# Forty instead of thirty-two tokens by gathered expert rows, with two VectorE dots in every body of the spread

## The reference

```python
q = (t @ w_pq).reshape(n_tok, 8, 2, 128)
sc = einsum('thcd,hckd->thck', q, sub_keys)            # 128 keys in each half
top_s, top_i = top_k(sc, 16)                            # then the 16 best of the 16 x 16 sums
expert_idx, gate = ...                                  # 8 heads x 16 picks of 16384 experts
a = gelu(einsum('thkd,td->thk', expert_u[expert_idx], t))
out = einsum('thk,thkd->td', gate * a, expert_v[expert_idx])
x = rms_norm(x + out)
```

## Time and profile before

| | |
|---|---|
| median of three runs | 2140.78 us |
| the profiled execution's own time | 2139.2 us |
| its span from first to last instruction | 2137.2 us |
| granted TensorE clock, mean | 0.997 |
| TensorE matmul busy | 2108.7 us (99%) |
| TensorE weight load busy | 1973.4 us (92%) |
| VectorE busy | 1584.1 us (74%) |
| ScalarE busy | 1118.9 us (52%) |
| GpSimd busy | 488.8 us (23%) |
| DMA, mean | 226 GB/s |

### The profile page before, as it was taken

The page is one execution under the profiler, slowest core; times in us unless marked ns, Lnnn a source line. Parts: engine busy times, 40 slices in busy tenths (PEclk is TensorE's granted clock), DMA queues, the critical chain, the costliest instruction groups (busy, mean ns, idle before and its releaser), DMA issues.

```text
span 2137.2 us, 40878 instructions
## 1 busy us (share of the span) xinstructions
PE 2108.7 (99%) x13494; PEld 1973.4 (92%) x13494; DVE 1584.1 (74%) x2622; ACT 1118.9 (52%) x1879; POOL 488.8 (23%) x379
## 2 busy tenths in 40 slices
PE   8999999999999999999999999999999999999997
PEld 6888888889989999999999999999999999999997
DVE  6555566667777986888778888888777776777775
ACT  5444455446455655556555555555555554555553
POOL 0000000000000000001999999332222220111110
PEclk9999999999999999999999999999999999999998
DMA  7655554445556556666767666888877776877773
GB/s 246 235 187 190 183 166 157 149 155 189 181 192 230 166 174 210 207 210 224 228 221 222 222 221 222 286 309 313 312 286 291 285 283 215 267 275 266 268 251 128
DMA packets 134750, 482.26 MB, mean 226 GB/s; under 512 B 15455, under 2 KB 18399, under 8 KB 134295
## 3 DMA queue, kind: packets, MB, share of 16 engines
q1 hardware_dynamic: 116072, 414.29, 57.6%
q0 software_dynamic: 18432, 67.12, 8.8%
q10 hardware_dynamic: 174, 0.05, 0.0%
HBM read 477.16 MB, written 4.24 MB: 225 GB/s over the span
## 4 chain that ended last, share of the span: by engine, by line
PE 95%; DVE 3%; issue 1%; DMA 1%; ACT 0%; DVEq 0%; SPq 0%; ACTq 0%
PE ps L1643 35%; PE ps L1912 19%; PE ps L1650 19%; PE ps L1916 11%; PE ps L1673 5%; PE ps L1896 2%; DVE lo L1014 1%; PE ps L1767 1%; PE ps L1749 1%; PE ps L1758 0%; DMA raw<-w_down 0%; DMA x_t<-x_t 0%; DVE score_b L1322 0%; DVE idx_now L1324 0%; DVE top_now L1328 0%
## 5 line engine op out<-in xcount | busy, mean ns | idle before, releaser
L1014 DVE TENSOR_TENSOR lo<-raw,hi 128x1024 fp32r<-128x1024 f32 x760 | 935.3, 1231 | 473.5 <-PE ps L1643 144.5
L622 ACT CAST hi<-raw 128x1024 fp32r<-128x1024 f32 x760 | 795.7, 1053 | 346.8 <-DMA raw<-w_down 137.6
L1643 PE MATMUL ps<-move_u,hi 128*128 128x448 f32 x2048 | 451.1, 368 | 0.0
L1912 PE MATMUL ps<-act_now,hi 128*128 128x448 f32 x2048 | 439.8, 365 | 0.4 <-ACT hi L622 0.4
L1912 PEld LDWEIGHTS ps<-act_now,hi 128*128 128x128 f32 x2048 | 375.0, 188 | 26.4 <-issue 0.7
L1643 PEld LDWEIGHTS ps<-move_u,hi 128*128 128x128 f32 x2048 | 371.0, 189 | 24.6
L1643 PE MATMUL ps<-move,hi 128*128 128x512 f32 x1536 | 379.3, 395 | 9.5 <-ACT hi L622 9.5
L1643 PEld LDWEIGHTS ps<-move,hi 128*128 128x128 f32 x1536 | 281.5, 189 | 62.9 <-issue 9.5
L630 ACT COPY upper<-ps 128x224 f32<-128x224 f32 (+1 forms) x224 | 80.3, 358 | 484.3 <-PE ps L1643 484.2
L602 POOL TENSOR_SCALAR one_j<-iota,j_t,gate_t 128x128 f32<-128x128 f32 x224 | 296.8, 1331 | 3.0 <-ACT j_t L880 1.8
L1916 PEld LDWEIGHTS ps<-act_now,lo 128*128 128x128 f32 x2048 | 250.6, 191 | 7.3 <-DVE lo L1014 2.0
(11 more groups left out here) (206 smaller groups left out, 1628.2 us busy)
## 6 DMA issues: line engine op xcount, KB each, us to landing
raw<-w_u SPq DMA_DIRECT2D x256, 512.0 KB
raw<-w_down SPq DMA_DIRECT2D x256, 512.0 KB
raw<-w_qk SPq DMA_DIRECT2D x68, 512.0 KB
raw<-w_gate SPq DMA_DIRECT2D x64, 512.0 KB
raw<-w_out SPq DMA_DIRECT2D x32, 512.0 KB
raw<-w_pq SPq DMA_DIRECT2D x32, 512.0 KB
raw<-w_v SPq DMA_DIRECT2D x28, 512.0 KB
raw<-w_o SPq DMA_DIRECT2D x24, 512.0 KB
```

Of the source, the lines that this page charges most:

```text
L622: nc.scalar.copy(hi[slot][:], raw[slot][:]).then_inc(hi_ready, 1)
L1014: nc.vector.tensor_tensor(lo[s % LOS][:], raw[s % RAW][:], hi[s % RAW][:].bitcast(F32), ALU.subtract).then_inc(lo_ready, 1)
L1643: ins = nc.tensor.matmul(ps[bank][:, 0:2 * w], hi[slot][:, col:col + P], m, start=begins, stop=ends)
L1912: return nc.tensor.matmul(ps[d][:, 0:2 * TD], hi[s % RAW][:, d * P:(d + 1) * P], act_now[s % ACTS][:], start=begins, stop=ends)
```

## The change

S becomes 40. That makes TD = 216, COPIES = 3 (three copies of 40 tokens, NP = 120 partitions), PICKS = 43 and STEPS = 86, PAIRS = 108 and UG = 51, so the spread has 27 bodies. A gather fetches 120 rows. Three `rows` buffers are used in turn instead of two. The dots stand in slot 3 of bodies 22 and 23, then in slots 1 and 3 of every body from 24 on, which is up to body 65, the second body of the down stage. GpSimd issues gather 2 before pair 0 and gather 3 before pair 1, and from then on gather g before pair 2g - 5, so two in every body of the spread. A gather of step g now waits for the dot of g - 3. The 43 adds of each half are spread out evenly up to its chunk 123: the first half from chunk 16 on (one every 2.55 chunks), the second from chunk 2 on (one every 2.88).

Picking the tokens' own indices is done by six small matmuls (for expert numbers and gates) instead of two, and ScalarE then needs two copies instead of eight. `fold` moves to another place in SBUF, and SP loads it after `move_free` instead of in the pq stage.

```diff
-S = 32
+S = 40
 TD = T - S
 COPIES = P // S
-PICKS = PH * TOPK // COPIES
+NP = COPIES * S
+PICKS = -(-PH * TOPK // COPIES)
+ROWS = 3
 STEPS = 2 * PICKS
...
+DOT_AT = [it * BODY + s for it in range(UR, (CHUNKS["u"] + CHUNKS["down"]) // BODY) for s in (1, 3)
+          if s == 3 or it >= U0][:STEPS]
+WEIGHED = DOT_AT[-1] // BODY + 1 - CHUNKS["u"] // BODY
...
+def row_before_pair(n):
+
+    return tuple(g for g in range(2, STEPS) if DOT_AT[g] < UG * BODY and max(0, DOT_AT[g] - U0 * BODY - 2) == n)
...
 def adds_of(c, half):
 
-    first, apart = (2, 7 / 2) if half else ((WEIGHED + 2) * BODY, 11 / 4)
+    first = 2 if half else (WEIGHED + 2) * BODY
+    apart = (HALF * BODY - 5 - first) / (PICKS - 1)
...
             def gather(table, n):
 
-                if table == "u_rows" and n >= 2:
-                    pool.wait_ge(dot_done, n - 1)
...
+                g = n + STEPS * (table == "w_down")
+                if ROWS <= g:
+                    pool.wait_ge(dot_done, min(STEPS, g - ROWS + 1))
...
             for n in range(PAIRS):
-                if n % BODY == 2:
-                    gather("u_rows", n // BODY + 2)
+                for g in row_before_pair(n):
+                    gather("u_rows", g)
                 if n >= 2 * TOGETHER:
                     pool.wait_ge(gates_spread, n - 2 * TOGETHER + 1)
...
-            for n in range(PAIRS // BODY + 2, STEPS):
-                gather("u_rows", n)
+            for n in range(STEPS):
+                if DOT_AT[n] >= UG * BODY:
+                    gather("u_rows", n)
...
             def dot_of(n):
 
-                v.wait_ge(row_landed[n % 2], 16 * (n // 2 + 1))
+                v.wait_ge(row_landed[n % ROWS], 16 * (n // ROWS + 1))
...
+            for q, own in enumerate(own_of):
+                nc.tensor.matmul(chosen[:, :, 0:own.stop - own.start], sel[:, q, :], e_pair[:, :, own],
+                                 start=q == 0, stop=q == COPIES - 1)
```

More of the change, by code:

```diff
@@ L366, in build @@
         e_pair = at("e_pair", ARENA + 98 * KB, [P, 2, P])
-        sel = at("sel", ARENA + 99 * KB, [P, P])
-        rows = [at(f"rows{i}", ARENA + (112 + 4 * i) * KB, [P, CW]) for i in range(2)]
+        sel = at("sel", ARENA + 96 * KB, [P, COPIES, NP])
+        rows = [at(f"rows{i}", ARENA + (112, 116, 108)[i] * KB, [P, CW]) for i in range(ROWS)]
         acc = at("acc", ARENA + 120 * KB, [P, D])
         idx = at("idx", MOVE + 31 * KB, [P, STEPS], U32)
[L371 to L374, removed]
+        dots = at("dots", MOVE + 31 * KB + 352, [P, STEPS])
+        gates_s = at("gates_s", MOVE + 31 * KB + 704, [P, PICKS])
+        w_s = dots[0:NP, 0:PICKS]
+        fold = at("fold", MOVE + 16 * KB + 2 * TD * 4, [P, S])
         x2 = at("x2", MOVE, [P, KT, T])
@@ L861, in gelu_and_index @@
                     a.wait_ge(e_turned, 1)
[L862 to L866, removed]
-                    ins.then_inc(idx_ready, 1)
+                    nc.scalar.copy(idx[0:NP, :], ps[7][0:NP, 0:STEPS])
+                    nc.scalar.copy(gates_s[0:NP, :], ps[7][0:NP, 2 * P:2 * P + PICKS]).then_inc(idx_ready, 1)
             for first, tt in ((1, 1), (EXP_AT[1] + 1, 0)):
@@ L1449, in dot_of @@
             def dot_of(n):
[L1451 to L1454 removed]
+                v.wait_ge(row_landed[n % ROWS], 16 * (n // ROWS + 1))
+                c, row = n // PICKS * CW, rows[n % ROWS][0:NP, :]
+                nc.vector.tensor_tensor_reduce(row, row, h_rows[0:NP, c:c + CW], 1.0, 0.0, ALU.mult, ALU.add,
+                                               dots[0:NP, n:n + 1]).then_inc(dot_done, 1)
             def dots_at(it, s):
@@ L1905, in _ @@
                     body("u", two * 2 + (U0 + k), before=spread_gates(k))
+            for it in range(UG - (UG - U0) % 2, UG):
+                body("u", it, before=spread_gates((it - U0) % 2))
             with pe.Fori(UG, CHUNKS["u"] // BODY) as it:
@@ L1966, in last_body @@
                 pe.wait_ge(row_added, PICKS * (half + 1))
+                pe.wait_ge(fold_in, 16)
                 for d in range(8):
-                    nc.tensor.matmul(ps[d][:, 2 * TD:2 * TD + S], acc[:, (8 * half + d) * P:(8 * half + d + 1) * P], fold[:],
+                    nc.tensor.matmul(ps[d][:, 2 * TD:2 * TD + S], acc[0:NP, (8 * half + d) * P:(8 * half + d + 1) * P], fold[0:NP, :],
                                      start=False, stop=False, skip_group_check=True)
@@ L2038, in columns, with own_copies @@
     return np.ascontiguousarray(b.reshape(-1, P, CW))
+def own_copies():
+    sel = np.zeros((P, COPIES, NP), np.float32)
+    for q in range(COPIES):
+        sel[P - S:, q, q * S:(q + 1) * S] = np.eye(S, dtype=np.float32)
+    return sel
 def weave(wa, wb):
```

62 lines of the change are left out of this document (30 added, 32 removed).

## The result

The change makes the kernel slower: 2207.98 us (median of 4, 2196.62 to 2214.92) against 2141.45 us (2140.64 to 2145.96), a ratio of 1.030 with the interval 1.025 to 1.035. The forecast was 2183 with a range up to 2202: the sign was right, the time lies 6 us above the range. The profiled execution took 2214.92 us, the slowest of the four, with a span of 2213.1. Of all executions of the experiments one, of e8, ran slow (2942.15 us at a granted clock of 0.654, its other nine at 0.994 to 0.997) and enters neither median nor ratio.

The account below looks back on a forecast made before the run. TensorE bounds the kernel now; afterwards GpSimd was to bound the spread. 2139.2 - 27.6 saved + 69.8 stalled = 2181.4 us for a profiled execution, 2183 as a median, range 2138 to 2202.

Parts of the forecast that it names:

- case A: In the spread, GpSimd becomes the bound at 13.7 to 15 us a body: 2183 us, range 2167 to 2200; chance 0.58.
- The stall: In the spread, TensorE waits for GpSimd, 69.8 us over the 27 bodies.
- 14.28: GpSimd's us per spread body: 6.26 for eight `one_j`, 2.46 for two gathers, the rest blocked behind VectorE's operations; TensorE needs 11.63.
- dot g - 3: In the spread, a gather's wait for this dot, with three row buffers, was to cost 0.
- rival D: Rows land too late for the dots, or gathers' waits close a ring around GpSimd, VectorE and TensorE: over 2200 us; chance 0.03.
- Everything behind the spread: After the spread, DMA stays at 313 GB/s, late loads cost TensorE 0 of 0 to 3 us, adds 0.
- B: In the spread, GpSimd is the bound but packs better, about 13.1 us a body: 2151 us, range 2137 to 2167; chance 0.22.
- C: In the spread, GpSimd's blocked time is slack, so only TensorE's saving is left: 2113 up to 2120 us; chance 0.17.
- TensorE's own sum: Over all matmuls, 27.6 us less: 26.7 from wide ones, 1.8 from fewer spread matmuls, minus 0.9 for index picking.
- the floor: Narrow matmuls already take a least time of 0.111 us each, so going from 224 to 216 columns saves 0.
- VectorE's share in the spread: VectorE's busy share in the spread was to be lower than before, as TensorE waits for GpSimd.
- The adds of the first half: Behind the spread, 86 adds at one per 2.55 chunks, 2.0 us a body against 1.9, were to cost 0.

Follow-up runs that it names:

- e8: Against e4: two dots in every third body of the spread (9 of 27), one in the others, 128 rows; 2142.26 us, ratio 0.9992.
- e4: Against the changed kernel: one dot and one gather in each body of the spread, and gathers of 128 rows; 2139.34 us, ratio 0.9991 to the kernel before.
- e1: Against the changed kernel: gathers of 128 rows instead of 120, the 8 extra rows unused; 2181.09 us, ratio 1.0194 to the kernel before.
- e6: Against e4: one more VectorE operation of a dot's form in each spread body, without a gather, and two row buffers instead of three; 2201.38 us.
- e7: Against e4: one more gather of 128 rows in each spread body, without a dot, and two row buffers instead of three; 2191.51 us.
- e11: Against e4: three dots in every body behind the spread instead of two; 2122.76 us, ratio 0.9922 to the kernel before.
- e3: Against the changed kernel: one dot and one gather in each body of the spread, still 120 rows; 2214.54 us, ratio 1.0350 to the kernel before.

## Why the prediction was wrong in its time and right in its sign

**The likeliest case A, GpSimd as the bound, held.** The stall was forecast at 69.8 us (added up from its own terms it is 69.6). Measured it is 377.0 in the changed kernel less 309.3 in e4, where nothing stalls: 67.7. GpSimd's `one_j` in the changed kernel and in e1:

```profile
L610 POOL TENSOR_SCALAR one_j<-iota,j_t,gate_t x216: 783/832/2998, 1008.9 to 1385.3; 128x128 f32<-128x128 f32 x108
L610 POOL TENSOR_SCALAR one_j<-iota,j_t,gate_t x216: 780/968/3615, 1008.9 to 1377.7; 128x128 f32<-128x128 f32 x108
```

With its last operation that is 377.2 us for 27 bodies in the changed kernel, 13.97 us each, forecast 14.28.

**Part of the closeness is luck.** 12 of the 67.7 us go away with 128 rows, so they aren't the stall that I forecast. In e1 the stall is 365.0 - 309.3 = 55.7 us, 14 less than forecast, and a body takes 13.7 us, at the lower edge of case A. That e1's 2181 us is so near 2183 all the same comes from small losses elsewhere that I had put at 0. An estimate from the rows: with 6.5 ns off each wide matmul (below) and one body more behind the spread, TensorE alone would need 442.0 us from the spread to the first fold, and e1 has 446.2; 319.3 from fold to fold, and e1 has 324.6; and 2.5 us are lost behind the last fold. With 0.6 ahead of the spread that is some 13 us, against the 14 that the stall was too large.

**The parts of the 14.28 were less right than their sum.** GpSimd between 1020 and 1320 us in the changed kernel:

```profile
L610 POOL TENSOR_SCALAR one_j<-iota,j_t,gate_t 128x128 f32<-128x128 f32 x171 | 228.9, 1346 | 2.3
L591 POOL DMA_INDIRECT rows<-u_rows,idx x42 | 50.3, 1196 | 19.0 <-DVE dots L1458 12.0 <-issue 7.0
```

Blocked are 8 x (1.346 - 0.783) = 4.5 us a body, not 5.56. Two gathers are 2.4 us, as forecast (2.46); but a wait stands beside them that I had put at 0, that for dot g - 3: 12.0 us over these 21 bodies, 0.6 a body. It is the ring of rival D in small: GpSimd late, so TensorE late, so `lo` and the dot late, so GpSimd's next gather late. One operation of a dot's form alone costs 1.0 us a body and one gather 0.5, and both together 2.1, half a us more than the sum. Two things on record are of that size: the wait for dot g - 3 (6.2 us of the 300 in e1, 0.3 a body, and none in e6 and e7), and a slack that gives way only once: GpSimd's record of a gather lasts 1.66 us in e4, where nothing stalls, and 1.25 in e6. No run separates them. Nor do I know exactly what the clock adds. In the stalled spread it was granted at 0.92 to 1.00, mean 0.96 from 1020 to 1320: by the trace's record of the clock it stood at its lower level, 1.2 GHz, for 31 of the 377 us, and at the upper, 2.4 GHz, for the rest. In e1 that was 14 of 365 us, in e4 none. A spread matmul's record is 578 ns at most in the changed kernel and 275 in e4. So, as an estimate, the lower clock can have cost TensorE at most half of those times, 15 and 7 us, and the difference could be a good part of the 12 us of e1.

**The step that failed is "Everything behind the spread", in its DMA term.** It counted bytes over time, 3.08 MB in 9.83 us, found "the same 313 now", and put what late loads cost TensorE at 0 of 0 to 3 us. The bytes were right. That 120 rows instead of 128 take more engine time for fewer bytes was not in it, although the change itself set the 120: 62 us of engine time for a MB instead of 46. From the spread to the first fold that is 470.4 - 446.2 = 24 us, and 12 more go with it in the spread. Between the profiled executions of the two kernels it is 34.9 us, between their medians 27, so up to 8 of the 24 and 12 belong to the executions that were profiled. The 27 us are about the distance from the forecast to the time, 25.

**Rivals.** B, 13.1 us a body, and C, TensorE's sum alone, fell with the spread's 377.0; with e1's 13.7 us a body B is nearer than it looked. C's slack exists, but at half a microsecond a body. D, over 2200 us, had the right time for the wrong reason: VectorE hardly waits for rows, its ring costs 0.6 us a body, and what lifts the time over 2200 are late loads of `w_u` and `w_down`.

**TensorE's own sum was right.** The chain of the kernel after, in the down stage:

```profile
1608.47 3.15 PE ps L1928 x16
1611.62 1.77 PE ps L1932 x16
```

Sixteen wide matmuls are 0.09 us shorter than in the earlier trace rows (forecast 0.11), but these rows are rounded to 0.01 us, which is 2.6 us over 4096 matmuls. The starts in the trace are finer: one wide matmul follows the other after 202.6 ns before and 196.2 ns in e11 (means of 300 to 700 in each of four stretches), 6.5 ns less, so 26.5 us over 4096, forecast 26.7. The narrow ones follow each other after 111.0 and 111.2 ns: the floor was right, nothing came back. The Trainium skill's formula ("TensorE: Matmul & The Clock Gate", "Back-to-back issue gap"), by which they would have given back 13.7 us in all, doesn't hold for them here. The section gives it for an isolated matmul and says itself that at few columns it counts too little, since the weight load is left out, so it was a weak rival from the start. e11, which stalls almost nowhere, has a span 22.7 us under that of the kernel before, 5 us short of that sum, of which 3.5 lie between spread and first fold (445.5 against the estimate of 442.0). **VectorE's share in the spread** was to be lower than before, and is: 295.23 of 377 us, 78%, where it was 272.62 of 327, 83%. The adds of the first half, taken at 0, cost little in e1 (TensorE is busy for 238.40 of 240 us there), and would have cost more with later dots.

**Behind the last fold** the changed kernel takes 3.1 us more than the kernel before. That is the clock. The last matmuls with `ones` in the changed kernel, and the same ones of the kernel before:

```profile
L2016 PE MATMUL ps<-ones,sq x32: 166/352/353, 2191.3 to 2201.0; 128*128 128x1 f32 x32
L1999 PE MATMUL ps<-ones,sq x32: 164/250/271, 2118.6 to 2125.2; 128*128 128x1 f32 x32
```

In the changed kernel the granted clock falls to 1.2 GHz 9.0 us behind the last fold, while these matmuls still run, before 15.3 us behind it. All thirteen traces go the same way: where it falls 8.9 to 9.8 us behind the fold (after, e1, e3, e4, e7, e8) the rest takes 28.4 to 29.3 us, and where it falls 13.9 us or more behind it, 25.8 to 26.2. Why it falls sooner in some no run shows.

**What stays open**: why 15 engines are dearer for a byte than 16; and how the 12 us of the spread that e1 gives back split between later loads and the clock.

## What to carry to other kernels

When a tile's rows change from 128 to another number, cost its DMAs by engine time and not by bytes, and look at the largest number up to 16 that divides the rows before the bytes: a few unused rows were worth 27 us here. An engine at 23% of the span can be the one that is full in the stage that the change loads, and what fills it may be another engine's operations. When work is taken out of a full stage, say where it goes: with 128 rows the same 27 dots and their gathers cost 56 us in the spread (e1), some 15 where they crowd the adds (e4 against e11 from spread to fold, 460.1 and 445.5 us), and little when they come three to a body right behind the spread (e11).

## What the hardware showed that I had not expected

- Gathers of 112, 120, 124 and 128 rows of 4 KB: 51, 60, 68 and 45 us of one DMA engine for a MB in the kernel before; with 124 rows 512 packets a gather, 388 of them small, 14.5 us to landing, and 2440 us for the kernel.
- The gathers on 120 rows slow the ordinary loads beside them: in the rest of u a 4 KB packet of theirs takes 219 ns in the mean, 191 with 128 rows, and the stretch moves 286 GB/s at a DMA share of 1.03 instead of 318 at 0.90.
- GpSimd's `one_j` grows from 1.227 to 1.408 us when VectorE runs one more operation with two SBUF inputs in a body, and shrinks to 1.150 when GpSimd itself has a gather more.
- The granted clock was 0.92 to 0.97 in five of the six parts of a spread in which TensorE waited up to 3.4 us at a time, so at 1.2 GHz for some of each and at 2.4 for the rest, and 1.00 in the spread of e4, where it had no gap.
- The stretch behind the last fold takes 26 or 29 us, by when the granted clock falls.
